# Memory keys and values beside the router, the last expert item written out behind the loop and fetched by column halves, in an fp32 transformer step on one core

## The reference, cut to what matters

```python
logits = (t @ router_w) + router_b
top_vals, top_idx = lax.top_k(logits, TOP_K); top_w = jax.nn.softmax(top_vals)
gates = sum(one_hot(top_idx, N_EXPERTS) * top_w[..., None], axis=1)
for e in range(N_EXPERTS):
    out = out + gates[:, e:e+1] * swiglu(t, w_gate[e], w_up[e], w_down[e])
```

```python
mh = rmsnorm_2(mem, g_mem_norm); mkv = mh @ w_mem_kv; mk, mv = split(mkv); mk = rmsnorm_2(to_heads(mk), g_mem_k)
```

## Time and profile before

| | |
|---|---|
| runs | 2020.28, 2020.41, 2022.66 us; median 2020.41 |
| the profiled execution | 2018.65 us |
| its span | 2016.8 us, granted TensorE clock 0.989 |
| busy share | PE 97%, PE weight load 80%, DVE 73%, ACT 62%, POOL 3% |
| moved by DMA | 521.21 MB, 258 GB/s on average |

### The profile page before, as it was taken

How to read it: one execution, slowest core, us unless ns; L and a number is a source line. 1 busy time by engine, 2 the same in 40 slices (tenths; PEclk the granted TensorE clock), 3 DMA queues, 4 the chain that set the end, 5 groups by cost and what they waited for, 6 DMA issues and landing times.

```text
span 2016.8 us, 25987 instructions
## 1 busy us (share of the span) xinstructions
PE 1948.0 (97%) x9376; PEld 1604.2 (80%) x9376; DVE 1476.3 (73%) x1282; ACT 1242.2 (62%) x1079; POOL 56.6 (3%) x97
## 2 busy tenths in 40 slices
PE   7999999898799999999999999999988999999999
PEld 6888877796588888888888888888866788788887
DVE  5554656676598898888889898888876656676554
ACT  5543557222477877777777777777765457645443
POOL 0000001000110000000000000000001100000000
PEclk9999999999899999999999999999999999999999
DMA  8954533003499999999999999999965442245452
GB/s 315 348 185 156 209 136 126 1 1 113 155 410 365 399 357 382 382 357 410 356 392 369 373 390 365 392 364 388 382 264 220 147 146 84 105 146 205 174 186 83
DMA packets 78069, 521.21 MB, mean 258 GB/s; under 512 B 8240, under 2 KB 10544, under 8 KB 18352
## 3 DMA queue, kind: packets, MB, share of 16 engines
q1 hardware_dynamic: 74752, 507.69, 65.4%
q0 software_dynamic: 3104, 12.06, 1.5%
q10 hardware_dynamic: 144, 0.52, 0.1%
HBM read 505.03 MB, written 15.20 MB: 258 GB/s over the span
## 4 chain that ended last, share of the span: by engine, by line
PE 73%; DVE 6%; ACT 3%; issue 1%; POOL 1%; DMA 1%; DVEq 0%; SPq 0%; ACTq 0%; POOLq 0%
PE bank L768 15%; PE bank L764 15%; PE bank L763 15%; PE bank L480 6%; PE bank L497 6%; PE bank L481 6%; PE bank L553 3%; PE bank L785 1%; DMA raw<-in_tiles_dram 1%; DVE w_lo L1713 1%; ACT w_hi L1209 1%; DVE w_lo L2012 1%; POOL small L1635 1%; DVE kT L1793 0%; PE bank L630 0%
## 5 line engine op out<-in xcount | busy, mean ns | idle before, releaser
L2012 DVE TENSOR_TENSOR w_lo<-raw,w_hi 128x2048 fp32r<-128x2048 f32 x339 | 769.2, 2289 | 118.4 <-ACT w_hi L1361 114.3
L1361 ACT ACTIVATE w_hi<-raw 128x2048 fp32r<-128x2048 f32 x339 | 648.3, 1918 | 148.0 <-PE bank L768 147.9
L1713 DVE TENSOR_TENSOR w_lo<-raw,w_hi 128x2048 fp32r<-128x2048 f32 (+2 forms) x136 | 297.7, 2198 | 169.3 <-ACT w_hi L1209 168.3
L1209 ACT ACTIVATE w_hi<-raw 128x2048 fp32r<-128x2048 f32 (+2 forms) x136 | 249.0, 1839 | 184.4 <-PE bank L497 168.0
L763 PE MATMUL bank<-w_hi,xT 128*128 128x512 f32 x896 | 356.1, 397 | 2.9 <-ACT w_hi L1361 2.8
L764 PE MATMUL bank<-w_hi,xT 128*128 128x512 f32 x896 | 351.6, 392 | 0.0
L480 PE MATMUL bank<-w_hi,xT 128*128 128x512 f32 (+1 forms) x784 | 314.0, 402 | 24.9 <-DVE xT L1744 9.1
L481 PE MATMUL bank<-w_hi,xT 128*128 128x512 f32 (+1 forms) x784 | 308.9, 396 | 0.0
L768 PE MATMUL bank<-w_lo,xT 128*128 128x512 f32 x896 | 241.9, 392 | 1.2 <-DVE w_lo L2012 1.2
L763 PEld LDWEIGHTS bank<-w_hi,xT 128*128 128x128 f32 x896 | 168.9, 189 | 38.8 <-ACT w_hi L1361 3.5
L768 PEld LDWEIGHTS bank<-w_lo,xT 128*128 128x128 f32 x896 | 168.2, 188 | 38.3 <-DVE w_lo L2012 1.6
(11 more groups left out here) (392 smaller groups left out, 1923.3 us busy)
## 6 DMA issues: line engine op xcount, KB each, us to landing
raw<-in_experts_dram SPq DMA_DIRECT2D x339, 1024.0 KB, 7.0
raw<-in_tiles_dram SPq DMA_DIRECT2D x125, 1024.0 KB, 4.8
rows_in<-zeros POOLq DMA_DIRECT2D x1, 6144.0 KB, 32.6
raw<-in_tiles_dram SPq DMA_DIRECT2D x9, 512.0 KB, 3.5
item_rows<-rows_in SPq DMA_DIRECT2D x8, 512.0 KB, 7.4
rows_out<-y_s SPq DMA_DIRECT2D x8, 512.0 KB, 3.4
rows_out<-zeros POOLq DMA_DIRECT2D x1, 1536.0 KB, 37.2
row<-in_rows_dram SPq DMA_DIRECT2D x1, 1040.0 KB, 14.8
```

The lines of the kernel that those rows point to most:

```text
L1209: nc.scalar.activation(w_hi[:, i % SPL, 0:kc * w], raw[:, i % DENSE, 0:kc * w], ACT.Copy)\
L1361: nc.scalar.activation(w_hi[:, j % SPL, :], raw[:, j % RAW, :], ACT.Copy).then_inc(m_hi, 1)
L1713: nc.vector.tensor_tensor(w_lo[:, i % SPL, 0:kc * w], raw[:, i % DENSE, 0:kc * w], w_hi[:, i % SPL, 0:kc * w], ALU.subtract).then_inc(spli ...
L2012: nc.vector.tensor_tensor(w_lo[:, j % SPL, :], raw[:, j % RAW, :], w_hi[:, j % SPL, :], ALU.subtract).then_inc(m_lo, 1)
```

## The change

1. **Memory keys and values.** The weight tiles of `mk` and `mv` come directly behind those of `dn_out` in the stream, interleaved. The memory is loaded before `dn_in` begins; ACT squares it in block 3 of deltanet (`norm_squares("mm", ...)`). PE turns it and computes mk and mv around the router. The results lie in `k_raw` and `v_mem` until the attention.
2. **dn_out** runs with its column halves interleaved, and the first half of `h` is turned inside its last tile. Six fillers stand behind the turn of the second half.
3. **Item 0** is no longer gathered by matmuls. POOL makes the normed rows (four operations of 128 x 1024) and scatters them as soon as `dest` is known, which DVE now computes before the loop; item 0 is read back from HBM like the others. SP loads three expert tiles after the memory has been turned, and the others behind the scatter.
4. **The last item** is written out behind the loop with `final=True`: it turns no next rows, and stores each column half by itself. The rows are fetched by column halves: half 0 while the last tiles are multiplied; its turn (m2) stands before the last tile. The gains of the final norm and of the second block's norm are multiplied once by POOL (`fin`, `mix`) and applied at the turn; the two roots are combined at the end.
5. **fxq and fxk** run with interleaved tiles (first tiles before, second tiles after the turn of half 1), and PE turns the heads of mk and fxq behind both.
6. All eleven items of `rows_out` are zeroed at the start, where three were.

```diff
@@ PE, experts
-                turn_norm("n3", h, after=(acc_free["D"], added(("dn_out", 0)), added(("dn_out", 1))))
+                turn_norm("n3", h, (1,), (acc_free["D"], 0, added(("dn_out", 1))))
+                keep_busy(6)
                 result(("n3", 3))
                 narrow_products("router", ROUTER)
+                pe.wait_ge(mem_loaded, 16)
+                turn_norm("mm", mem_in, (0,))
                 narrow_turned("router", ROUTER)
-                keep_busy(6)
+                turn_norm("mm", mem_in, (1,))
+                begin(mk, "A")
+                tile(mk, 0, xT1, xT2, turned="mm")
...
+                begin(mv, "A")
+                tile(mv, 0, xT1, xT2, turned="mm")
+                tile(mk, 1, xT1, xT2, turned="mm")
+                tile(mv, 1, xT1, xT2, turned="mm")
+                pe.wait_ge(m_rows, 16)
+                for half in range(2):
+                    b = tp_bank(("first", half), "D")
...
+                        last = nc.tensor.transpose(b[:, k * P:k * P + P], item_rows[:, ch * P:ch * P + P], ident)
@@ PE, the last tile of the last item, and behind it
+                        if final and f == FB - 1:
+                            turn_norm("m2", h, (0,), (h_half, 1))
                         product(j, hidden(f), acc[3][:, :], f == 0, f == FB - 1)
...
-                turn_norm("mm", lambda tt, ch: mem_in[tt][:, ch, :])
-                keep_busy(4)
-                gemm(("b_in", "mk"), "A", xT1, xT2, turned="mm")
-                gemm(("b_in", "mv"), "A", xT1, xT2)
-                pe.wait_ge(h_done, 6)
-                turn_norm("m2", h)
+                begin(fxq, "A")
+                tile(fxq, 0, xT1, xT2, turned="m2")
+                begin(fxk, "A")
+                pe.wait_ge(m_y, last_one * 2 + 3)
+                tile(fxk, 0, xT1, xT2, turned="m2")
+                turn_norm("m2", h, (1,), (h_half, 1, 2))
+                tile(fxq, 1, xT1, xT2, turned="m2")
+                tile(fxk, 1, xT1, xT2, turned="m2")
@@ SP
+            sp.wait_ge(tp_done, batch_of["mm", 3][1])
+            sp.wait_ge(rows_zero, 32)
             for j in range(RAW):
+                s = raw_slot(j)
...
+                if s == 0:
+                    sp.wait_ge(dispatched, 16 * TOP_K * NT)
+                    sp.dma_start(item_rows[:, :], rows_in[0]).then_inc(m_rows, 16)
                 load_expert(j, 0)
...
+            ahead = 2
+            for c in range(2):
+                store_half(c)
+                for i in range(NA + (ahead if c else 0), NA + (DENSE if c else ahead)):
+                    sp.wait_ge(m_lo, last * MT + (MT - DENSE + i % DENSE + 2))
+                    load(range(i, i + 1))
@@ ACT, deltanet
+                    if c == 3:
+                        act.wait_ge(mem_loaded, 16)
+                        norm_squares("mm", mem_in, mem_junk[:, :])
@@ POOL
+            for tt in range(NT):
+                own(nc.gpsimd.tensor_tensor(xn[:, tt, :], h[:, tt, :], R("scale"), ALU.mult))
+                tell(nc.gpsimd.tensor_tensor(xn[:, tt, :], xn[:, tt, :], root("n3", tt).broadcast_to((P, D)), ALU.mult),
+                     xn_rows)
...
+            pool.wait_ge(y_last[0], 16)
+            for j in range(TOP_K * NT):
+                collect(0, j)
+            for j in range(0, TOP_K * NT, TOP_K):
+                collect(1, j)
+            pool.wait_ge(y_last[1], 16)
+            for j in range(1, TOP_K * NT, TOP_K):
+                collect(1, j)
@@ DVE, second_block
+                combine(0, 0)
+                combine(0, 1)
+                split_to(NA + 1)
+                norm_turn("m2", "final", halves=(0,))
+                split_to(NA + 2)
+                combine(1, 0)
+                split_to(NA + 3)
+                combine(1, 1)
+                norm_turn("m2", "final", halves=(1,))
+                split_to(NA + 4)
```

More of the change, by code:

```diff
@@ L149, in weight_stream @@
         put(dn_in[c])
-    for c in range(2):
-        put(block(("dn_out", c), "dn_w_out", c * CB, CB, D))
+    put(*(block(("dn_out", c), "dn_w_out", c * CB, CB, D) for c in range(2)))
+    put(block(("b_in", "mk"), "w_mem_kv_2", 0, CB, D), block(("b_in", "mv"), "w_mem_kv_2", CB, CB, D))
     before_experts = len(pieces)
[L153 to L156, removed]
+    b_in = [block(("b_in", name), "w_in_2", c0, CB, D) for name, c0 in B_IN]
+    put(*b_in[:2])
+    for b in b_in[2:]:
+        put(b)
     for b, c in GATES:
@@ L736, in experts @@
                 nc.tensor.matmul(b[:, 16:24], C("ones"), sel[1], start=False, stop=True).then_inc(tp_done, 1)
-                def gather(b, half):
+                begin(mv, "A")
[5 more added lines that the diff above has]
+                    b = tp_bank(("first", half), "D")
                     for k in range(4):
                         ch = 4 * half + k
[L742 to L751, removed]
+                        last = nc.tensor.transpose(b[:, k * P:k * P + P], item_rows[:, ch * P:ch * P + P], ident)
+                    last.then_inc(tp_done, 1)
+                result(("first", 1))
                 for o in "AD":
@@ L802, in experts @@
                             product(j, tokens(j), u, j % 2 == 0, j % 2 == 1)
-                    pe.wait_ge(m_rows, i * 16 + 16)
-                    for half in range(2):
+                    if not final:
+                        pe.wait_ge(m_rows, i * 16 + 32)
+                    for half in range(0 if final else 2):
                         pe.wait_ge(m_read, i * M_BANKS + (4 + half))
@@ L1649, in _ @@
             tell(nc.gpsimd.memset(zeros[:, :], 0.0), zeros_set)
+            pool.wait_ge(first_in, 16)
+            fin, mix = (col[:, COL_AT[n][0]:COL_AT[n][1]] for n in ("final", "mix2"))
+            own(nc.gpsimd.tensor_tensor(fin, fin, mix, ALU.mult))
             for tag in ("n0", "n1"):
@@ new lines, in _ @@
+            for j in range(0, TOP_K * NT, TOP_K):
[3 more added lines that the diff above has]
+                collect(1, j)
+            norm_root("fin")
+            ss, v, y, u = (cells("m2", j) for j in range(4))
+            y_fin = cells("fin", 2)
+            pool.wait_ge(sq_done, 2 * (NORMS.index("m2") + 1))
+            own(nc.gpsimd.tensor_tensor(u, y_fin, y_fin, ALU.mult))
+            own(nc.gpsimd.tensor_tensor(v, ss, u, ALU.mult))
@@ L1964, in experts @@
                      route_dve)
-                one = rt[:, R_ONE:R_ONE + TOP_K * NT, :].rearrange("p (t k) e -> p t k e", t=NT)
-                for k in range(TOP_K):
-                    own(nc.vector.tensor_scalar(one[:, :, k, :], rt[:, R_RANK:R_RANK + 2, :], float(k), None, ALU.is_equal))
+                split_to(end + 1)
+                norm_turn("mm", "mem2", halves=(1,))
+                split_to(end + 2)
                 b = batch("places")
@@ new lines, in experts @@
+                far = float(2 * MAX_ITEMS * P)
+                own(nc.vector.scalar_tensor_tensor(out=mine[:, :, 0, :], in0=sel, scalar=far, in1=where, op0=ALU.mult,
+                                                   op1=ALU.subtract))
+                own(nc.vector.tensor_tensor(mine[:, :, 1, :], sel, where, ALU.mult))
+                to = dest_f[:, :].rearrange("p (t k) -> p t k", t=NT)
+                own(nc.vector.tensor_reduce(to, mine, AX, ALU.max))
+                own(nc.vector.tensor_scalar(to[:, :, 0], to[:, :, 0], -1.0, far, ALU.mult, ALU.add))
@@ new lines, in experts @@
+                tell(nc.vector.tensor_copy(dest[:, :], dest_f[:, :]), dest_ready)
+                split_to(end + 3)
+                own(nc.vector.memset(item_f[:, :], 0.0))
+                own(nc.vector.tensor_copy(item_f[:, 0:NE], C("iota")[:, 0:NE]))
+                own(nc.vector.tensor_reduce(item_f[:, 13:14], cnt, AX, ALU.add))
+                own(nc.vector.tensor_scalar(item_f[:, 13:14], item_f[:, 13:14], float(NE - 1), None, ALU.add))
+                ind = rt[:, R_IND:R_IND + more, :]
@@ L2035, in experts @@
+                own(nc.vector.tensor_reduce(item_f[:, NE:NE + more], rt[:, R_TMP:R_TMP + more, :], AX, ALU.add))
+                tell(nc.vector.tensor_copy(item_i[:, :], item_f[:, :]), items_ready)
                 dve.wait_ge(route_act, 1)
```

423 lines of the change are left out of this document (230 added, 193 removed).

## The result

The changed kernel takes 2044.38 us (median of four runs, 2043.56 to 2046.14) against 2020.97 for the kernel before (four runs, 2020.28 to 2022.66): a ratio of 1.0116, interval 1.0098 to 1.0133. It is slower by 23.4 us where 5.7 us faster was forecast, and outside the range. The profiled execution took 2044.02 us with a span of 2042.2.

A forecast was written before the change was run, and what follows sets the result against it. PE was taken to bound the loop, with time to win only in waits, fillers and slow stretches. Terms 2.4 + 12.7 + 0.1 - 20.9 = -5.7 us took 2020.41 to 2014.7 us, range 2004.5 to 2024.

The forecast's parts named there:

- The step that failed: Whole kernel: products are conserved, so only waits, fillers and slow stretches change the time; a tile costs 2.75 us.
- the rivals: Item 0's rows late (2027.7 us, chance 0.14); second fetch still slow (2022.0, 0.12); more cover (2007.2, 0.22).
- Deltanet, +2.4: Deltanet: the memory's squares on ACT delay the squares PE waits for, +2.4 us, between 0 and 3.5.
- the wait of about 4 us for the sum of squares: Deltanet: PE waiting about 4 us there was to show the prediction right; 1.46 us before.
- Router and loop, +12.7 and +0.1: Router: first expert product at 552, +12.7 us (+9 to +26). Loop: turn dropped, code entry added, +0.1.
- the 1 us for the hold-up: Router: 1 us added for POOL and DVE holding each other up, within +12.7.
- rival B: Router: busy DVE holds POOL up, item 0's rows come late and it starts at 566; 2027.7 us, chance 0.14.
- the 558.7: Router: a first expert product from about 558.7 was to decide against the change, for late rows of item 0.
- The up to 4 us: Router: ranking on DVE could wait up to 4 us for POOL's row operations, making the sum -2.7.
- entry cost of the second code copy: Loop's last item: entering a second copy of the instructions costs 0 to 2 us, taken as 1.
- the late splits of the old entry: Loop entry: 1.6 us lost to late splits before should go, since three tiles are split ahead.
- Tail, -20.9: From the last expert tile's start: `fxq` heads at +50.4, not 73.7, less 2.4 at half clock; -24 to -10.

The follow-up runs named there:

- the old distance: Changed kernel with its buffers laid out so that tokens and hidden units stand from the weights as in the kernel before (-64): 2019.49 us, ratio 0.9987.
- the pair at distance 0: Kernel before with 64 unused bytes behind the columns of gains, 2012.87 us; changed kernel with 32 unused bytes there, 2009.41 us.
- the pair at -32: Kernel before with 32 unused bytes behind the columns of gains, 2047.12 us; changed kernel as first run, 2044.38 us.

## Why the prediction was wrong, point by point

**The step that failed** stands in the first part: "All products are conserved; only waits, fillers and slow stretches can change the time", with the unit behind it, a tile of 2.75 us. The products were conserved in number, and each of some 7080 became up to 4.4 ns longer. The eight new columns moved the stationary operands from -64 to -32 modulo 256 against the weights. That cost 24.9 us (2044.38 against 2019.49 with the old distance), of which the loop has 16.7 (969.75 against 953.05 us from the first product to the end of the last tile but one). None of the rivals had it; a column of gains looked free because it adds no instruction.

**Deltanet, +2.4**: the size is right, and the place is not. From the turn of n2 to the sum of squares the stage grows from 90.17 to 92.53, by the pairs at distance 0 and -32 also by 2.4 (90.09 to 92.48, 90.83 to 93.20), and moving the squares away gives it all back. But the wait of about 4 us for the sum of squares, the sign that the prediction named, did not come: it is 2.15 us, and was 1.46. Most of the rest is a wait for ACT's split of a weight tile, which stands on ACT right behind the squares of the memory. The prediction had put ACT's delay on the wrong wait, and only the sum came out right.

```profile
306.41 0.47 PE L499 MATMUL bank<-w_hi,xT 128*128 128x512 f32 x1 [1.59 <-ACT w_hi L1257]
...
320.68 8.77 PE L649 MATMUL bank<-squares,cst 128*16 128x256 f32 x32 [2.15 <-ACT squares L1362]
```

The sum of squares itself takes 8.77 us here against 7.08 in the earlier trace rows. That is not shown to be the change's: the kernel before at distance 0 takes 8.76 for it (wait 2.22, granted clock 0.56 in its first 3 us), and the changed kernel without the row products 7.08 (wait 2.22, clock 1.00). From there to the turn of `o` the pair here differs by 3.3 us, those at distance 0 and -32 by 0.2 and 0.5.

**Router and loop, +12.7 and +0.1**: measured +17.8 and -3.1, together 14.7; by the pair at distance 0 17.2, by the pair at -32 15.7. So the term is 2 to 4 us short. The first expert product follows the turn of `o` by 74.7 us, where the working gives 56.9 + 13.3 = 70.2, and 71.2 with the 1 us for the hold-up. In the prediction's count that is 556.5, between my 552 and rival B's 566 and short of the 558.7 that was to decide for B. And of B's mechanism, POOL held up to 5.5 us per operation, nothing came: POOL's four took 2.39, 1.89, 2.39 and 2.03 us, and it was DVE that waited.

Step by step, at the distance of the kernel before, the working was off so. `dest` came 1.5 us late: ranking took 5.3 us, 2.7 of them hold-up, but it began 1.0 us earlier than worked out. The scatter's last issue ended 4.1 us later still, since the issues took 2.43, 0.96, 0.95 and 3.02 us, 8.3 with their gaps where 5.1 was taken, and began 0.9 us behind `dest`; the first and the last of them began while DVE ran a split, and ended 0.8 to 1.0 us behind that split. Landing and read took 5.8 us, 2.4 less than worked out. And from the transposes to the first product it took 4.8 us, not 3.5, with another split of ACT (1.91 us) ahead of it. So the mis-sized terms are the hold-up of DVE by POOL, taken at 1 and measured at 2.7 at `dest` and 3.4 at the product, and the issues of the scatter. The rule of the Trainium skill (SBUF — State Buffer, section Who interferes with whom), that a VectorE operation with two SBUF inputs and a GpSimd operation reading SBUF wait for each other, was right to weigh in: the trace agrees, with 1.28 and 1.87 us for operations that take 0.17 and 0.29 alone. The up to 4 us that the prediction worked out beside it was nearer than the 1 that it took.

Nothing showed an entry cost of the second code copy: the loop is 3.1 us shorter, by the other pairs 2.1 and 1.9. Of that 0.9 are the turn left out, and 1.2 to 1.5 the late splits of the old entry, which I had put to the router.

**Tail, -20.9**: right in the mechanism, with luck in the sum. From the start of the last tile to the heads of `fxq` 52.0 us instead of 73.9, and 0.75 us given back behind them: -21.1. The wait ahead of the last tile was forecast at 1.7 and is 1.77 to 1.86; there is the idle stretch of 10 us ahead of the heads, released by DVE. But the heads, forecast at +50.4, are at +52.0, and the 2.4 us that were to be lost behind them are 0.75: two misses of 1.6 us that cancel. Two more were wrong and hardly mattered. The first fetch's issues took 1.8 to 2.5 us each beside the splits, not 1.3. And the last rows of half 1 landed at about +20, not +18 (DVE, itself behind a split whose tile had come late, idles 0.8 us for them), so that PE turned the second half of `h` at +20.9, not at +19.4.

**The sum**: 5.7 us forecast for these terms, some 2.5 measured at equal distance. Added up from the traces, the same terms (deltanet up to the sum of squares, router, loop, tail) give -4.0 here, -1.1 at distance 0 and -6.0 at -32, so single executions scatter by as much as the effect. The sign was right for what the prediction reasoned about, and wrong for the kernel that was run.

## What to carry to other kernels

When every instruction of one form changes its length, from the first stage on and at the same granted clock, look at what the change did to addresses, not to order: compare the step between two equal passes in both traces first. A product of 128 x 512 in `fp32r` here wants its stationary and its moving operand at the same remainder modulo 256 bytes within the partition; fix the layout (pad small buffers) before judging a change of the order, since the layout is worth more (2009 to 2045 us for one program) than most such changes. And compare orders only at equal layout.

## What the runs showed of the hardware, unexpected

- The pace of `fp32r` products of 128 x 512 depends on the distance of their operands in SBUF: 226.7 ns each at 0 modulo 256 bytes, 228.9 at -64, 233 at -32, 32, 64 and 128. No other distance was tried. Moving both by 32 bytes changes nothing. What in the chip makes it so was not shown.
- A tile in which one operand of three stands at another distance is slow nearly throughout (2.79 us against 2.75 by pairs).
- An operation of VectorE on 16 columns took 1.28 us and one on 128 columns 1.87 us beside GpSimd's products of 1024 columns; with these cut to two columns, 0.17 and 0.29.
- An indirect DMA took GpSimd 0.94 to 0.97 us to issue when VectorE was idle, had short operations, or took tokens out of PSUM. One that began while a split of VectorE ran (two operands in SBUF) ended 0.8 to 1.0 us behind the end of that split, and so took 1.2 to 3.1 us. One of 0.96 us, at 549.38 in the kernel before, began 0.15 us ahead of a split and was not held up. No run tested the cause by itself.
